# Seven products of summed half blocks for the ups of seven pairs in the first block's feed-forward layers

## The reference, cut to what matters

```
# first model, each of 2 layers, behind the attention part
x = _layernorm(ALPHA * x + y, ln1_g[l], ln1_b[l])
f = (jax.nn.silu(x @ w_gate[l]) * (x @ w_up[l])) @ w_down[l]
x = _layernorm(ALPHA * x + f, ln2_g[l], ln2_b[l])
...
# second model, twice in each of 2 layers, with halves added to the residual
def swiglu(x, w_gate, w_up, w_down):
    return (jax.nn.silu(x @ w_gate) * (x @ w_up)) @ w_down
```

## Time and profile before

| what | value |
|---|---|
| median of 3 runs | 3109.06 us (3108.43 to 3110.61) |
| the profiled execution | 3107.27 us |
| its span, first to last instruction | 3105.5 us |
| mean granted clock of TensorE | 0.998 |
| PE busy | 3076.8 us, 99% of the span |
| DVE busy | 1738.1 us, 56% |
| POOL busy | 1837.9 us, 59% |
| ACT busy | 923.1 us, 30% |

### The profile page before, as it was taken

The page is one execution under the profiler, slowest core; times in us unless marked ns, Lnnn a source line. Parts: engine busy times, 40 slices in busy tenths (PEclk is TensorE's granted clock), DMA queues, the critical chain, the costliest instruction groups (busy, mean ns, idle before and its releaser), DMA issues.

```text
span 3105.5 us, 46781 instructions
## 1 busy us (share of the span) xinstructions
PE 3076.8 (99%) x17462; PEld 2646.5 (85%) x17462; DVE 1738.1 (56%) x2750; ACT 923.1 (30%) x1800; POOL 1837.9 (59%) x2485
## 2 busy tenths in 40 slices
PE   8999999999999999999999999999999999999999
PEld 7878998898789988899887789988899887789987
DVE  5576545275765452866527567661667336567641
ACT  4454222054542220622212332220323022332210
POOL 5346447673364476544978374478545977374494
PEclk9999999999999999999999999999999999999999
DMA  5112322231123322232332123223222332122231
GB/s 187 48 42 82 108 102 95 95 107 44 42 82 108 106 98 89 75 108 101 102 112 89 48 82 108 102 95 102 95 98 98 103 111 89 41 96 104 92 110 67
DMA packets 83062, 284.53 MB, mean 92 GB/s; under 512 B 9531, under 2 KB 15068, under 8 KB 82652
## 3 DMA queue, kind: packets, MB, share of 16 engines
q1 hardware_dynamic: 77484, 273.70, 26.0%
q10 hardware_dynamic: 5424, 8.79, 0.8%
HBM read 278.79 MB, written 3.67 MB: 91 GB/s over the span
## 4 chain that ended last, share of the span: by engine, by line
PE 94%; DVE 3%; ACT 2%; issue 0%; DMA 0%; DVEq 0%; ACTq 0%
PE bank_v L591 21%; PE bank_v L593 20%; PE bank_v L592 20%; PE bank_s L867 6%; PE bank_s L869 6%; PE bank_s L868 6%; PE bank_a L591 2%; PE bank_a L593 2%; PE bank_a L592 2%; PE bank_v L993 1%; PE bank_a L972 1%; PE bank_s L1133 1%; PE bank_s L1011 1%; PE bank_v L1148 1%; DVE t_sum L2146 0%; PE bank_s L1136 0%
## 5 line engine op out<-in xcount | busy, mean ns | idle before, releaser
L565 POOL TENSOR_TENSOR w_lo<-raw,w_hi 128x512 fp32r<-128x512 f32 x808 | 1085.6, 1344 | 64.6
L591 PE MATMUL bank_v<-xn_hi,w_hi 128*128 128x512 f32 (+1 forms) x1680 | 641.3, 382 | 8.0 <-DVE xn_lo L1934 8.0
L592 PE MATMUL bank_v<-xn_lo,w_hi 128*128 128x512 f32 (+1 forms) x1680 | 635.1, 378 | 0.0
L593 PE MATMUL bank_v<-xn_hi,w_lo 128*128 128x512 f32 (+1 forms) x1680 | 634.8, 378 | 0.0
L561 POOL TENSOR_TENSOR zero<-zero 128x1 f32<-128x1 f32 x808 | 250.0, 309 | 569.0 <-PE bank_v L593 421.0
L562 POOL CAST w_hi<-raw 128x512 fp32r<-128x512 f32 x808 | 545.2, 675 | 0.1
L591 PE MATMUL bank_v<-h_hi,w_hi 128*128 128x512 f32 (+1 forms) x1122 | 422.9, 377 | 0.0
L593 PE MATMUL bank_v<-h_hi,w_lo 128*128 128x512 f32 (+1 forms) x1122 | 422.5, 377 | 0.0
L592 PE MATMUL bank_v<-h_lo,w_hi 128*128 128x512 f32 (+1 forms) x1122 | 422.5, 377 | 0.0
L554 POOL TENSOR_TENSOR zero<-zero 128x1 f32<-128x1 f32 x54 | 28.5, 529 | 602.4 <-DVE w_lo L2189 602.4
L591 PEld LDWEIGHTS bank_v<-xn_hi,w_hi 128*128 128x128 f32 x1680 | 316.7, 189 | 66.1 <-issue 8.7
(11 more groups left out here) (413 smaller groups left out, 6419.4 us busy)
## 6 DMA issues: line engine op xcount, KB each, us to landing
raw<-in_w_stream SPq DMA_DIRECT2D x516, 512.0 KB, 3.3
rope<-in_rope ACTq DMA_DIRECT2D x2, 1024.0 KB, 6.2
da_v<-t_rows ACTq DMA_DIRECT2D x2, 1024.0 KB, 7.1
out<-resid SPq DMA_DIRECT2D x8, 256.0 KB, 2.3
t_rows<-t_row ACTq DMA_DIRECT2D x1, 1536.0 KB, 7.2
resid<-in_x ACTq DMA_DIRECT2D x5, 256.0 KB, 7.1
mla_v<-in_alibi ACTq DMA_DIRECT2D x2, 512.0 KB, 6.6
resid<-in_x SPq DMA_DIRECT2D x3, 256.0 KB, 9.3
```

The lines of the kernel that those rows point to most:

```text
L565: ins = pool.tensor_tensor(w_lo[:, u, cut], raw[:, u, cut], w_hi[:, u, cut].bitcast(F32), ALU.subtract)
L591: pe.matmul(out, lhs_hi, rhs_hi, start=first, stop=False)
L592: pe.matmul(out, lhs_hi, rhs_lo, start=False, stop=False)
L593: return pe.matmul(out, lhs_lo, rhs_hi, start=False, stop=last)
```

## The change

1. **Ups in seven products.** In "ffn" alone (`UPS_PAIRED`), the ups of pairs 1 to 7 are seven products as well, of the same token sums (`side_products(..., "up", ...)`). The ups of the first and the ninth pair stay plain. On PE a pair of the loop is now two sides of 84 matmuls of 256 columns each; POOL splits nothing in these pairs, and DVE and ACT make sums, high and low parts for both sides. The loop is taken apart: a pair "zero", a loop over pairs 1 to 6 (in the second block 1 to 7), "seven" and "last".
2. **The order on DVE.** In all feed-forward layers the next side's four sums stand directly behind u3 and ahead of c22 (`behind("u3")`). S1 is written over A21 in the raw unit. S4 is written to a bank of PSUM that is idle there (`bank_a`), in the first pair into raw unit a.
3. **Low parts.** The order is S2 with S3, a, b (S1 and A22 as one instruction of 1024), S4. A raw slot is given back when all four are done, and not before S4's any more.
4. **Scaling.** In `ffn_scaled` the ups are not scaled when `hidden` is written; one multiply of gate and bank writes it. `down` scales instead: each chunk has two dependent instructions (`add_half`), bank x 0.5 x `scale_by` into `work`, then the add to `resid`. c21 and c22 are scaled together. In pair zero ACT keeps p1 ahead of the silu of the last plain gate.

```diff
-LO_PARTS = ("a", "S23", "S1", "A22", "S4")
+LO_PARTS = ("S23", "a", "b", "S4")
+UPS_PAIRED = ("ffn",)
+        for side in range(2 if tag in UPS_PAIRED and 0 < j < PAIRED - 1 else 1):
+            PAIRED_UNITS[start + 2 * PLAIN + 4 * j + 2 * side] = len(PAIRED_UNITS)
...
+        def last_sum_place(tag, at, side):
+            return raw[:, side_slots(tag, side)[0], KEPT:UNIT] if at == "first" else bank_a[SIDES.index(side)][:, :]
...
-                    pool.wait_ge(weights_lo.sem, len(LO_PARTS) * GATE_UNITS[n] + RAW_FREE)
+                    pool.wait_ge(weights_lo.sem, len(LO_PARTS) * (PAIRED_UNITS[n] + 1))
+                    pool.wait_ge(w_split.sem, split_count(n - 1))
                     pool.tensor_tensor(zero[:, 2:3], zero[:, 0:1], zero[:, 0:1], ALU.add).then_inc(w_split.sem, 2)
...
+                side_products(tag, "zero", "gate", 0)
+                plain_ups("zero")
+                if tag in UPS_PAIRED:
+                    with loop(pe, tag, PAIRED - 3) as i:
+                        for side in SIDES:
+                            side_products(tag, "pair", side, i + 1)
+                    for side in SIDES:
+                        side_products(tag, "seven", side, PAIRED - 2)
+                else:
+                    with loop(pe, tag, PAIRED - 2) as i:
+                        side_products(tag, "pair", "gate", i + 1)
+                        plain_ups("pair")
+                side_products(tag, "last", "gate", PAIRED - 1)
+                plain_ups("last")
...
+            def weight_sums(tag, at, side, j):
+                dve.wait_ge(raw_in[a].sem, side_raw(tag, side, j))
+                dve.wait_ge(raw_in[b].sem, side_raw(tag, side, j))
+                dve.tensor_tensor(total[:, 1, :], w11, w21, ALU.subtract)
...
+                dve.tensor_tensor(w21, w21, w22, ALU.add)
...
+                dve.tensor_tensor(total[:, 0, :], w21, w11, ALU.subtract)
...
+                    last_sum(tag, at, side)
...
+            def combine_22(key, c22, behind=lambda name: None):
...
+                dve.tensor_tensor(u3, u2, bank_21, ALU.add).then_inc(*combined.done((*key, "u3")))
+                behind("u3")
+                dve.wait_ge(*multiplied.after((*key, "p5")))
+                dve.wait_ge(*combined.after((*key, "u3")))
+                dve.tensor_tensor(c22, u3, bank_12, ALU.add).then_inc(*combined.done((*key, "c22")))
...
+                    def behind(name):
+                        if name == "u3" and more:
+                            weight_sums(tag, at, "gate", j + 1)
...
-                    dve.scalar_tensor_tensor(out=resid[:, c, :], in0=v_bank(key)[:, :], scalar=0.5,
-                                             in1=resid[:, c, :], op0=ALU.mult, op1=ALU.add).then_inc(*v_read.done(key))
+                step(dve.scalar_tensor_tensor(out=work[:, 3, cut], in0=v_bank(key)[:, cut], scalar=0.5, in1=scale_by[:, cut],
+                                              op0=ALU.mult, op1=ALU.mult), (*key, "scaled"))
+                dve.tensor_tensor(resid[:, key[2], cut], resid[:, key[2], cut], work[:, 3, cut], ALU.add
+                                  ).then_inc(*v_read.done(key))
```

More of the change, by code:

```diff
@@ L879, in gate_products @@
+                key = (tag, at, side)
+                if side == "up":
+                    pe.wait_ge(*c11_read.after((tag, at, "gate", "c11")))
+                else:
+                    pe.wait_ge(*c11_read.before((*key, "c11")))
+                    if tag in UPS_PAIRED and at != "zero":
+                        pe.wait_ge(*(up11_read.after((tag, "seven", "up", "c11")) if at == "last" else
+                                     up11_read.before((tag, at, "up", "c11"))))
                 split("a")
-                multiply(bank_11, w11, x11).then_inc(*multiplied.done((tag, at, "p1")))
+                multiply(bank_11, w11, x11).then_inc(*multiplied.done((*key, "p1")))
@@ L887, in gate_products @@
+                split("b")
+                pe.wait_ge(*c12_read.before((*key, "c12")))
                 pe.wait_ge(*x_lo.after((tag, "t", 0)))
[L888 to L891, removed]
+                multiply(bank_12, s1, t1).then_inc(*multiplied.done((*key, "p5")))
@@ L897, in gate_products, with plain_ups @@
-                multiply(bank_12, s4, x22, True, {0: half_used.done((tag, at, "gates"), 2), 1: w_used.done((tag, at, "gates"), 2)}
-                         ).then_inc(*multiplied.done((tag, at, "p3")))
+                pe.wait_ge(*combined.after((*key, "c22")))
+                multiply(bank_12, s4, x22, True, {0: half_used.done((*key, "units"), 2), 1: w_used.done((*key, "units"), 2)}
+                         ).then_inc(*multiplied.done((*key, "p3")))
             def ffn_paired(tag):
-                with loop(pe, tag, PAIRED - 1) as i:
-                    gate_products(tag, "pair", i)
+                def plain_ups(at):
@@ new lines, in gate_side @@
+                        hidden_hi_early(tag, "p7", H_ORDER[0:4])
+                    else:
+                        sums_hi(tag, at, "gate")
+                    act.wait_ge(*multiplied.after((*key, "p2")))
+                    act.wait_ge(*combined.after((*key, "c22")))
+                    act.activation(work[:, 0, HALVES[0]], bank_11, ACT.Silu).then_inc(*c11_read.done((*key, "c11")))
+                    if at == "last":
+                        hidden_hi_early(tag, "p5", H_ORDER[4:6])
+                        hidden_hi_early(tag, "p4", H_ORDER[6:8])
+                    else:
+                        a_hi(tag, at, "gate", j + 1)
+                        act.wait_ge(*multiplied.after((*key, "p4")))
+                        b_hi(tag, at, "gate")
@@ L1599, in ffn_scaled, with gate_half @@
+                    if at != "last":
+                        act.wait_ge(*multiplied.after((*key, "p3")))
+                        last_sum_hi(tag, at, "gate")
+                def gate_half(at):
+                    key = (tag, at, "gate")
+                    act.wait_ge(*value.after((*key, "c12")))
+                    act.activation(work[:, 0, :], work[:, 0, :], ACT.Silu).then_inc(*gated.done((*key, 0)))
                 if kept:
@@ L1609, in ffn_scaled @@
                     first_pair_hi(tag)
-                gate(1, 1)
-                with loop(act, tag, PAIRED - 1) as i:
-                    pair("pair", i)
-                pair("last", None)
-                hidden_hi_rest(tag, ready)
+                gate_out(1, 1)
+                all_pairs(tag, gate_side, gate_half)
             def write_sink(key, n, k):
```

541 lines of the change are left out of this document (308 added, 233 removed).

## The result

The changed kernel takes 3116.35 us (median of 14 runs, 3114.78 to 3117.6), the kernel before 3108.22 us in the runs beside it. The ratio is 1.0026, with an interval of 1.0018 to 1.0034: 8 us, 0.26%, slower. The forecast was 3109.8 with a range to 3118. The time is in the range, but it is 6.5 us above the number, and the median has crossed the bound of 0.2% to "slower", to which I had given 0.18; the interval reaches down to 0.18%, so the crossing itself is not certain.

The account below looks back on a forecast made before the run. PE, busy 99% of the span, was taken to bound the kernel. The terms -11.5 + 6.2 + 2.6 + 3 + 0.45 = +0.75 on 3107.27 gave 3108.0; with the median 1.8 higher, 3109.8 us, range 3100.5 to 3118.

Parts of the forecast that it names:

- the bound of 0.2%: Whole kernel: a change within 6.2 us counts as the same; chances 0.62 same, 0.2 faster, 0.18 slower.
- PE's products, -11.5: Loops of "ffn": each pair of ups made seven products saves PE 0.82 us, 14 in two layers, -11.5 us.
- The four sums in the loops, nothing: Loop sides, 54 in all: four sums ahead of c22 cost nothing, as 0.5 us is left before p3.
- Pair zero of "ffn", +6.2: Both layers: raw units land late, sums take 1.1 us each, p3 waits 3.1 us; bounds 1.2 to 4.7 each.
- The rule on POOL and DVE: Pair zero of "ffn": POOL's SBUF reads may block all four sums, putting the wait near 4.7; forecast kept 1.1 per sum.
- Second block: Its pairs zero: first "ffn1" waits 5 us against 2.5 before, +2.6; three other layers 1.0 each, +3.
- The end, +0.45: End of down: the last half chunk's second scaling instruction, 0.42 us, and the hand-over are exposed, +0.45 us.
- what PE saves in the loops it waits away in pairs zero: Whole kernel: the forecast's closing sum, -11.5 + 6.2 + 2.6 + 3 + 0.45 = +0.75 us.
- my +0.75: Whole kernel: net change forecast on the profiled execution's 3107.27 us, giving 3108.0, or 3109.8 as median.
- waits in the loops: Loop sides: c22 late, 0.5 us in 28 sides of the second block, +14, 3124 us; chance 0.13.
- pairs zero at their upper bounds: Pairs zero: sums blocked throughout, net +8.4, 3117.4 us; chance 0.05 that it passes 6.2 us.

## Why the prediction was right in part, and wrong in one step

- **PE's products, -11.5.** Right: 11.2 and 12.3 us between pairs of runs that differ in this alone, 11.8 in the loops' periods, and 20.13 us a pair in the loop.
- **The four sums in the loops, nothing.** Right: 0.62 us to spare, no wait. The run with two more sums showed that the spare is not larger than that.
- **Pair zero of "ffn", +6.2.** Right in mechanism, low by 1.1: 3.75 and 3.55 us. In layer 0 undisturbed sums took what I said and two were stretched, but the second unit landed 5.6 us behind its issue, where the row of before had 4.3, so DVE began 3.1 us behind u3's end and not 1.8. In layer 1 it landed after 4.1 us, close to that row; there the sums were the error, one every 1.3 us where I had 1.1. The rows are of layer 0 and of layer 1:

```profile
DMA to landing us min/median/max: 3.4/4.5/5.6
...
DMA to landing us min/median/max: 3.2/3.6/4.1
```

- **The rule on POOL and DVE.** The Trainium skill (SBUF — State Buffer, "Who interferes with whom") had them exclude each other. The runs agree: 0.98 and 1.65 us with POOL at work, 0.69 and 0.70 without. By the rule taken to its end the wait would have been near 4.7. In layer 1, where all four sums were stretched, it was 3.55, less than that since the units came earlier than the bound had them.
- **Second block.** The first "ffn1" waits 1.4 + 4.2 = 5.6 us, where I had 5 in all; the three others 1.5, 0.8 and 1.6 us, together 3.9, where I had 3.
- **The end, +0.45.** From the start of the last chunk's last matmul to the end of the span it is 9.73 us after (3105.67 to 3115.4) and 9.06 before (3096.44 to 3105.5): +0.7, of which the second instruction's 0.46 is the term (it starts at 3106.44, the first at 3105.98).
- **The step that failed** is the sum itself: it ended "what PE saves in the loops it waits away in pairs zero", as if a wait of PE cost its length. It had no term for the clock. In its sum PE ran at full speed on both sides of a wait, and the only waits of the seven products that it had rows for, 1.9 and 0.6 us, had left the clock at 1.00 in that stretch. Waits of 3.55 to 4.2 us did not. That was most of 7.3 us in the profile (PE busy fell 4.2 us instead of 11.5): about 6.6 for the clock, the rest for the stops, and the run with a busy PE gave 6 back. Between the two profiles the sum is -11.5, +14.1 of time without work and +7.3, together 9.9, which is the difference of their spans; the medians differ by 8.1. So the waits too came out 1.9 longer than my terms, and it is chance that my +0.75 with 7.3 alone would meet the medians.
- The Trainium skill (TensorE: Matmul & The Clock Gate, "What's actually happening") says that PE's clock is by default the lower one and that activity releases it. The run with a busy PE agrees with that: the same late c22, the clock 1.00 with filler and 0.83 to 0.91 without it. I had not weighed that page against the waits I forecast.

That the time was in the range is luck in part: the range reached so far for the upper bounds of the waits, not for the clock that carried the time there. Of the 0.18 for "slower", 0.13 stood for waits in the loops, which did not come, and 0.05 for pairs zero at their upper bounds.

## What to carry to other kernels

A wait of the engine that bounds the program can be priced twice: its length, and what the clock takes from the work behind it. Here waits of 3.5 to 4.2 us cost 1.6 to 2.5 us more by the clock, those of 0.8 to 1.6 us in pairs zero nothing (the last section has other places), so one wait of 4 us cost more than several of 1. Every stop cost some 0.2 us beside what the list of waits shows, so the period of a loop says more than the list. When work is put ahead of something that the bounding engine waits for, look at the first pass of each loop apart, since there the inputs are late although the steady passes have room. And a change that pays in the steady state but loses at its edges can be split: here the gain of the ups came through with the old order kept in six places.

## What the runs showed of the hardware that was not expected

- Two units issued 0.37 us apart landed 3.4 and 5.6 us behind their issue in layer 0 of the change, 3.2 and 4.1 in layer 1, 3.3 and 4.3 in layer 0 before; the second one's time was no constant.
- The clock behind the waits: 0.84, 0.91 and 0.83 over the three windows with waits of 3.75, 3.55 and 4.2 us. Over 35 us from 3 us before pair zero of "ffn" on, the clock was 0.90 and 0.95 in the two layers of the change, and 0.95 and 0.95 in the run with plain ups, whose waits there were 3.7 and 3.5. So waits of the same length do not always cost the same.
- In the run with POOL held back, a wait of 2.6 us was followed by a dip (0.92 in the first window), and waits of 1.2 us in the run with the earlier give-back by none.
- The clock fell elsewhere too, and not in every execution: in the kernel before it was 0.57 from 828 to 832 us and 0.66 from 1278 to 1283, behind waits of 0.6 to 1.3 us; in the change it was 1.00 from 800 to 840, and in the run with a busy PE 1.00 from 1260 to 1283, behind waits of the same lengths. So a wait alone did not settle the clock, and what decides between such cases stays open.
